# Six weight copies of an output projection, moved from GpSimd to ScalarE

## The reference, cut to what matters

```python
y = jnp.concatenate([o_a, y_b], axis=-1) @ w_out      # the output projection, 1024 x 1024
...
x = x + gate1 * y
h = rmsnorm(x, norm_ffn_g[layer]) * (1 + scale2) + shift2
x = x + gate2 * conv_ffn(h, w_ffn_gate[layer], w_ffn_up[layer], ffn_conv[layer], w_ffn_down[layer])
```

## Time and profile before

| | |
|---|---|
| median of three runs | 1492.41 us |
| the profiled execution | 1494.65 us |
| its span in the trace | 1492.9 us |
| mean granted TensorE clock, share of 2.4 GHz | 0.975 |
| PE busy | 1406.8 us (94%) |
| DVE busy | 967.6 us (65%) |
| POOL busy | 498.7 us (33%) |
| ACT busy | 411.3 us (28%) |
| share of the chain that ended last: PE, DVE, ACT, DMA | 83%, 7%, 4%, 2% |

### The profile page before, as it was taken

One profiled execution on the slowest core, in us unless ns is written; L12 is line 12 of the kernel. 1 busy time (PEld: TensorE's weight loads), 2 busy tenths in 40 slices (PEclk: granted clock), 3 DMA queues, 4 the chain that ended last, 5 costly groups with the idle time before them and its releaser, 6 DMA issues.

```text
span 1492.9 us, 24317 instructions
## 1 busy us (share of the span) xinstructions
PE 1406.8 (94%) x9461; PEld 1367.8 (92%) x9461; DVE 967.6 (65%) x1388; ACT 411.3 (28%) x719; POOL 498.7 (33%) x300
## 2 busy tenths in 40 slices
PE   5899999999797999999999999879999999999996
PEld 3799899999697999999999999768999999999995
DVE  4565789886765778778888885357773255325554
ACT  4425443473514323012201321443110011001122
POOL 0000110005143333653355334203454455445452
PEclk8899999999898999999999999989999999999998
DMA  9433212632222235334334432112322222222222
GB/s 386 184 114 112 71 43 85 216 109 96 75 99 84 99 126 204 127 134 148 123 135 150 155 109 74 47 39 65 118 98 72 83 70 68 74 83 70 74 69 82
DMA packets 43685, 163.21 MB, mean 109 GB/s; under 512 B 4848, under 2 KB 6000, under 8 KB 42096
## 3 DMA queue, kind: packets, MB, share of 16 engines
q1 hardware_dynamic: 43632, 162.52, 31.3%
HBM read 154.12 MB, written 6.82 MB: 108 GB/s over the span
## 4 chain that ended last, share of the span: by engine, by line
PE 83%; DVE 7%; ACT 4%; issue 3%; DMA 2%; SPq 0%; ACTq 0%; POOL 0%; DVEq 0%; POOLq 0%
PE ps L683 73%; PE ps L994 2%; DMA ada_first<-in_w_ada 1%; PE ps L735 1%; ACT work L1215 1%; ACT work L1064 1%; PE ps L816 1%; DVE wlo L1586 1%; PE ps L948 1%; PE ps L946 1%; PE ps L936 1%; PE ps L786 1%; DMA work<-in_zeros 1%; DVE qkv L1669 1%; PE ps L806 1%
## 5 line engine op out<-in xcount | busy, mean ns | idle before, releaser
L683 PE MATMUL ps<-hhi,whi 128*128 128x320 f32 x1952 | 451.0, 312 | 20.3 <-DVE hlo L1514 18.2
L683 PE MATMUL ps<-hlo,whi 128*128 128x320 f32 x1952 | 446.8, 310 | 0.0
L683 PE MATMUL ps<-hhi,wlo 128*128 128x320 f32 x1952 | 446.7, 310 | 0.0
L683 PEld LDWEIGHTS ps<-hhi,whi 128*128 128x128 f32 x1952 | 328.4, 189 | 27.3 <-issue 18.3
L683 PEld LDWEIGHTS ps<-hlo,whi 128*128 128x128 f32 x1952 | 328.5, 189 | 0.0
L683 PEld LDWEIGHTS ps<-hhi,wlo 128*128 128x128 f32 x1952 | 328.3, 189 | 0.0
L604 POOL TENSOR_TENSOR wlo<-raw,whi 128x1024 fp32r<-128x1024 f32 (+1 forms) x100 | 251.0, 2510 | 8.3
L601 POOL TENSOR_SCALAR whi<-raw 128x1024 fp32r<-128x1024 f32 (+1 forms) x100 | 103.7, 1037 | 401.0 <-PE ps L683 358.8
L609 POOL TENSOR_TENSOR wlo<-raw,whi 128x1024 fp32r<-128x1024 f32 x44 | 109.9, 2498 | 214.5 <-ACT whi L1418 214.5
L683 PE MATMUL ps<-hidhi,whi 128*128 128x320 f32 x704 | 160.5, 309 | 0.0
L683 PE MATMUL ps<-hidlo,whi 128*128 128x320 f32 x704 | 160.4, 309 | 0.0
(11 more groups left out here) (209 smaller groups left out, 1404.0 us busy)
## 6 DMA issues: line engine op xcount, KB each, us to landing
raw<-in_w_gu SPq DMA_DIRECT2D x88, 512.0 KB, 3.3
ada_raw<-in_w_rows SPq DMA_DIRECT2D x70, 512.0 KB, 3.4
raw<-in_w_in SPq DMA_DIRECT2D x28, 512.0 KB, 3.3
raw<-in_w_dn SPq DMA_DIRECT2D x32, 448.0 KB, 3.2
ada_first<-in_w_ada SPq DMA_DIRECT2D x4, 2048.0 KB, 20.5
raw<-in_w_dn SPq DMA_DIRECT2D x16, 512.0 KB, 3.3
row_late<-in_w_rows SPq DMA_DIRECT2D x10, 512.0 KB, 3.3
raw<-in_w_out SPq DMA_DIRECT2D x8, 512.0 KB, 4.4
```

What stands on the lines that cost most here:

```text
L683: last = nc.tensor.matmul(pair[pr][:, b], wt[s][:, cs], act[:, k, b * HALF:(b + 1) * HALF], start=(j == 0 and q == 0), stop=(j == len(tile ...
```

## The change: what it does

The hi copies of out units 2 to 7 go from GpSimd to ScalarE. GpSimd's loop over these units keeps the subtracts alone. On ScalarE the loop over the eight squares is written out, and the copy of out unit k+2 stands directly ahead of square k, for k = 0 to 5:

```diff
@@ GpSimd
-            split_pairs(u, 4, first=1)
+            split_lo_pairs(u + 2, 3)
@@ ScalarE
-            squares_after(1, "out")
+            b = SEG["out"]
+            for k in range(KD):
+                if k + 2 < KD:
+                    weight_hi(b["u"] + k + 2)
+                act.wait_ge(s_ev["CB"[k % 2]], b["CB"[k % 2]] + k // 2 + 1)
+                act.wait_ge(s_acc, k + 1)
+                nc.scalar.activation(sq[k % 2], x[:, k, :], ACT.Square).then_inc(s_sq, 1)
```

## The result

The changed kernel takes 1497.72 us (median of 10 runs, 1495.82 to 1500.52) against 1493.73 for the kernel before (10 runs beside it, 1492.03 to 1494.88): a ratio of 1.0028, 95% interval [1.0019, 1.0037], so slower by 2.8 to 5.5 us. Three later comparisons of the same two kernels gave 1.0038 [1.0024, 1.0051], 1.0034 [1.0022, 1.0046] and 1.0036 [1.0023, 1.0049]. Over all 27 runs of the changed kernel the median is 1498.35; it varies more from run to run than the kernel before. Its profiled execution took 1500.52, the longest of its ten, with a span of 1498.7 against 1492.9.

What follows compares the result with a forecast made beforehand. PE was taken to bound the kernel (94% busy, 83% of the chain of waits). 1492.4 us plus 4.2 for a PE stall, 2.0 for the clock and 0 for removed GpSimd copies gave 1498.6, range 1495.4 to 1500.4.

Steps and rivals of the forecast that it cites:

- the likeliest case: Out stage: late load of unit 4 stops PE 4.2 us, then half clock costs 2.0; 1498.6 us, chance 0.75.
- Copy of unit 2 holds nothing.: ScalarE, ahead of square 0: copy done about 417.3, so square 0 at 417.57 and the subtract at 417.43 don't move.
- Square 1 behind the copy of unit 3.: ScalarE: square 1 waits for that copy, running at 429.15 instead of 424.43, 4.7 us later.
- Add 1 falls into the subtract.: VectorE: add 1 overlaps GpSimd's subtract of unit 3, ending at 432.33, 0.68 us after it.
- Row tile 23 and unit 4's load.: SP: row tile issued at 434.64 instead of 428.34, the load behind it at 435.01 instead of 428.71, 6.3 us late.
- The stall.: PE ahead of out unit 4: start at 443.04 instead of 438.84, +4.2 us; bounds 3.4 to 4.7, less without add-subtract overlap.
- The clock.: PE after standing still ahead of unit 4: granted clock falls to 1.2 GHz, costing +2.0 us; bounds 0 and 2.4.
- Units 5 to 7 follow without a pause, and all behind shifts rigidly.: PE after unit 4: later splits are ready in time, so no further gap; square 7, the norm and the rest just shift.
- the hold: ScalarE: square 1 held behind the copy of unit 3, which waits for that unit's load; absent in a rival of 0.08.
- not slower: Rival on ScalarE: unit 3's weights land early enough that no square is held; 1490.8 to 1492.4 us, chance 0.08.
- the clock did fall: Against the rival that PE stays at 2.4 GHz after its 4.2 us idle ahead of unit 4: 1496.6 us, chance 0.13.
- second stall: Rival: VectorE's backlog holds square 3, and that the copy of unit 6; another 6.2 us, 1504.8 us, chance 0.04.

Runs made afterwards that it cites:

- the gap was filled: Changed kernel with seven, then four matmuls of constants put ahead of out unit 4 on PE: 1498.98 us (1.0045), then 1498.15 (1.0035); four again 1497.62 (1.0029).
- the kernel with the hold alone: Changed kernel with the copies back on GpSimd; ScalarE only waits, ahead of square k, for the hi copy of unit k+2: 1500.59 us, ratio 1.0039.

## Why the prediction was right

Forecast 1498.6, range 1495.4 to 1500.4; measured 1497.72, and 1498.35 over all runs. That the number came so near is in part luck. The loss was forecast as 6.2 us and measured as 4.0 in the first comparison (5.0, 5.0 and 5.9 in the later ones); but it had been added to 1492.41, the median of three runs, and ten runs beside the changed kernel gave 1493.73. The mechanism isn't luck: the likeliest case is the one that came, link by link:

- *Copy of unit 2 holds nothing.* Copy at 416.49, square 0 at 417.69, as said.
- *Square 1 behind the copy of unit 3.* Forecast 429.15, came at 428.87. The copy began at 427.90, as its weights landed (issue at 423.40, 4.5 us); I had given ScalarE the 0.26 us that GpSimd took.
- *Add 1 falls into the subtract.* Forecast to end 0.68 after it, at 432.33; the subtract ended at 429.04 + 2.38 = 431.42 and the add at 432.09, 0.67 after. The Trainium skill's page "SBUF — State Buffer", section "Who interferes with whom", gives a reason: a VectorE instruction with two inputs in SBUF contends with a GpSimd one that reads SBUF, for ports that are locked to one of them at a time, while ScalarE never waits for another engine. The trace agrees: the add takes 2.47 us against 0.83, the subtract, which began first, keeps its 2.38, and ScalarE's copies take 1.06 wherever they fall.
- *Row tile 23 and unit 4's load.* Forecast 434.64 and 435.01, came at 434.41 and 434.79.
- *The stall.* Unit 4 was to start 4.2 us later than before. It started at 442.73 instead of 438.84, 3.89 later, of which 0.29 was there when the stage began: 3.6. This term was over-sized, by ScalarE's quicker start at two copies and slightly shorter landings.
- *The clock.* Forecast +2.0. Units 4 to 7 took 30.71, 30.64, 29.96 and 30.66 us in four profiles against 28.44 before, so 2.27, 2.20, 1.52 and 2.22. That work at half clock costs half its time was a little too dear: of the 5.07 us it cost 2.28, since 19 such matmuls take 2.79 at full clock (0.147 each). The Trainium skill's page "TensorE: Matmul & The Clock Gate", section "Why this matters for your kernels", warns of idle gaps between bursts of matmuls for this reason. The trace agrees: 0.50 after 3.9 us, 1.00 after 1.08, and 1.00 again when the gap was filled.
- *Units 5 to 7 follow without a pause, and all behind shifts rigidly.* So it was: 6.06 us at 494.27, with the long run of matmuls as long as before (459.64 against 459.65), and 5.8 at the end of the span.

So the sum was 3.6 + 2.3 = 5.9 us in the stage instead of 6.2. The runs' medians lie lower, +4.0 to +5.9; the profiled execution was the longest of the first ten.

Of the rivals, the hold came, so *not slower* fell; the clock did fall; no second stall came (square 3 at 448.71, the copy of unit 6 at 452.41, released by PE, as worked out).

## What to carry to other kernels

An instruction put into an in-order queue brings its wait with it, and everything behind it waits too. The time it takes is the smaller question: ask what stands behind it, who waits for that, and whether the path ends in a load whose landing the same instruction waits for. A queue of loads is such a place: a load that waits for another engine's result shouldn't stand ahead of one that PE needs. And a PE stall may cost more than its length, by the clock after it.

## What the runs showed of the hardware

- ScalarE began two copies within 0.1 us of the landing of their data (at 427.90, the load issued at 423.40 and 4.5 us under way; at 439.00, issued at 434.79 and 4.2 under way), GpSimd 0.26 us after it (428.11 against 427.85, and 427.34 against 427.07 in the kernel with the hold alone).
- After stalls of 3.8 to 4.0 us, alike but for 0.2 us, the granted clock stayed at 0.50 for 3.4 us of matmuls in one profile of the changed kernel and 5.1 us in another, so the same stall cost 1.52 to 2.27 us more; in the kernel with the hold alone units 4 to 7 took 31.11, 2.67 more. The changed kernel's runs spread over 6.2 us and those of before, beside them, over 3.4; in the four profiles this makes 0.75 us of it, and 3.0 lay ahead of the stage, as said above.
- At 1.2 GHz a matmul of 128x320 followed the one before it in 0.267 us (5.07 / 19), at 2.4 GHz in 0.147 (7.05 / 48): 1.8 times, not 2.
- A float32 matmul of 128x512 constants is two instructions and 0.86 us at full clock (seven of them: 14 instructions in 6.01 us).
